# Moving a weight fold, reordering one down projection and unsharing the last norm in an eight-core encoder step

## The reference, cut to what matters

```python
# 1: mixer
proj = rmsnorm(x, g_mix_pre) @ w_in
merged = [group_rmsnorm(pool(proj)), group_rmsnorm(conv(proj))]
x = x + rmsnorm(merged @ w_out, g_mix_post)
# 2: cross-attention into 256 memory tokens, 4 heads of 256
q = rmsnorm(x, g_x_pre) @ w_q
p = softmax(q @ k.T / 16); o = p @ v
x = x + rmsnorm(o @ w_co, g_x_post)
# 3: MLP
hid = square(relu(rmsnorm(x, g_ff_pre) @ w_up))
x = x + rmsnorm(hid @ w_down, g_ff_post)
```

## Time and profile before

| what | us |
|---|---|
| time, median of 3 runs | 868.41 |
| lowest and highest of the 3 | 868.3, 869.23 |
| the profiled execution's own time | 868.5 |
| its span on the slowest core (core 2), first to last instruction | 867.0 |
| spans of the eight cores | 851.2 to 867.0 |
| PE busy on core 2 | 820.3 (95%) |
| DVE busy, ACT busy | 386.4, 386.5 (45% each) |

### The profile page before, as it was taken

One profiled execution on the slowest core, in us unless ns is written; L12 is line 12 of the kernel. 1 busy time (PEld: TensorE's weight loads), 2 busy tenths in 40 slices (PEclk: granted clock), 3 DMA queues, 4 the chain that ended last, 5 costly groups with the idle time before them and its releaser, 6 DMA issues.

```text
span 867.0 us, 13886 instructions; the slowest of 8 cores (851.2 to 867.0 us)
## 1 busy us (share of the span) xinstructions
PE 820.3 (95%) x4724; PEld 393.3 (45%) x4724; DVE 386.4 (45%) x526; ACT 386.5 (45%) x804; POOL 112.6 (13%) x192
## 2 busy tenths in 40 slices
PE   2979999999979999999998999999999999999995
PEld 0444454444445454445454445444444444444442
DVE  3796875667766556666223213231222321222112
ACT  3486775848656476566332223341323411233111
POOL 7735105206010000200010000000000000000000
PEclk9999999999989999999999999999999999999998
DMA  8999259640099325893889724982148920194001
GB/s 187 201 229 176 76 196 208 102 62 1 3 153 163 116 81 200 140 173 80 145 146 161 179 73 113 158 148 75 73 118 150 154 67 25 53 154 86 25 25 49
DMA packets 29793, 102.39 MB, mean 118 GB/s; under 512 B 2386, under 2 KB 13266, under 8 KB 24348
## 3 DMA queue, kind: packets, MB, share of 16 engines
q0 software_dynamic: 19696, 68.37, 45.7%
q1 hardware_dynamic: 9884, 33.01, 11.1%
q10 hardware_dynamic: 144, 0.13, 0.1%
HBM read 144.38 MB, written 18.07 MB: 187 GB/s over the span
## 4 chain that ended last, share of the span: by engine, by line
PE 81%; DMA 9%; DVE 3%; issue 3%; POOL 2%; ACT 1%; another core or an unknown queue 0%; DVEq 0%; SPq 0%; POOLq 0%; ACTq 0%
PE ps L657 79%; DMA wdn_139<-w_down 4%; PE ps L662 2%; DMA wco<-w_co 2%; DMA win<-w_in 1%; DMA up_130<-w_up 1%; POOL sAB_100 L695 1%; DMA X<-x 1%; DVE pld_103 L712 1%; POOL sAB_101 L695 1%; ACT rf_107 L686 0%; DMA yp<-X 0%; DVE z_98 L693 0%; DVE X L712 0%
## 5 line engine op out<-in xcount | busy, mean ns | idle before, releaser
L657 PE MATMUL ps<-xT_53,win 128*128 128x512 bf16 x256 | 63.1, 390 | 16.9 <-DMA win<-w_in 15.8
L693 DVE TENSOR_TENSOR O_55<-ps,gp 128x1024 f32<-128x1024 f32 (+1 forms) x25 | 29.4, 1178 | 95.8 <-PE ps L657 74.7
L693 DVE TENSOR_TENSOR O_56<-ps,gp 128x1024 f32<-128x1024 f32 x24 | 29.3, 1222 | 95.1 <-PE ps L657 59.0
L686 ACT ACTIVATE rt_128<-ps 128x512 bf16<-128x512 f32 x64 | 38.2, 597 | 71.2 <-PE ps L657 69.0
L686 ACT ACTIVATE rt_127<-ps 128x512 bf16<-128x512 f32 x64 | 38.2, 596 | 70.5 <-PE ps L657 68.7
L686 ACT ACTIVATE O_55<-ps 128x1024 f32<-128x1024 f32 (+2 forms) x27 | 25.4, 942 | 94.2 <-PE ps L657 89.8
L686 ACT ACTIVATE O_56<-ps 128x1024 f32<-128x1024 f32 (+1 forms) x25 | 24.9, 996 | 94.2 <-PE ps L657 92.8
L657 PE MATMUL ps<-xT_54,win 128*128 128x512 bf16 x256 | 59.6, 379 | 0.0
L657 PEld LDWEIGHTS ps<-xT_53,win 128*128 128x128 bf16 x256 | 24.5, 100 | 45.4 <-issue 21.9
L657 PE MATMUL ps<-xT_54,up_129 128*128 128x512 bf16 x192 | 42.4, 379 | 0.0
L657 PE MATMUL ps<-xT_53,up_130 128*128 128x512 bf16 x192 | 42.4, 379 | 0.0
(11 more groups left out here) (333 smaller groups left out, 1506.2 us busy)
## 6 DMA issues: line engine op xcount, KB each, us to landing
up_129<-w_up POOLq DMA_DIRECT2D x11, 1024.0 KB, 9.8
up_130<-w_up POOLq DMA_DIRECT2D x11, 1024.0 KB, 10.0
up_131<-w_up POOLq DMA_DIRECT2D x10, 1024.0 KB, 9.9
x<-X SPq DMA_DIRECT2D x16, 512.0 KB, 3.4
X<-x SPq DMA_DIRECT2D x16, 512.0 KB, 4.3
yp<-X SPq DMA_DIRECT2D x15, 512.0 KB, 2.7
X<-xp POOLq DMA_DIRECT2D x8, 512.0 KB, 44.1
X<-xp SPq DMA_DIRECT2D x8, 512.0 KB, 4.1
```

Source lines behind the costliest of these rows:

```text
L657: P.add([("pe", lambda e, L: e.matmul(L(out), lhsT=lhsT, rhs=rhs, start=start, stop=stop, skip_group_check=True), max(0.03, n * 0.000421 + ...
L686: return e.activation(out=L(out), in_=L(in_), func=func, scale=scale, **kw)
L693: opts.append(("dve", lambda e, L: e.tensor_tensor(out=L(out), in0=L(in0), in1=L(in1), op=op), c_dve(n, per)))
```

## The change

Five edits go together:

- `load_win(0)` is recorded ahead of the four XT loads.
- `fold_b` moves from ahead of the attention loop to behind the four `attn_head` calls of its first pass (`p == 0`).
- In tile 0 of the MLP `out_tile` gets `late=True`: for sub-tiles 0 and 1 the first 16 k-chunks (both halves) run first, then the remaining 16 of sub-tile 0, then those of sub-tile 1; k-chunks go outside, halves inside. Sub-tiles 2 and 3 run over all 32 in one go, in that same loop order.
- From the attention stage on, ACT's squares in `post` and `post_halves` are written to a bfloat16 buffer of their own (`sqj`, over se0 and se1) in place of O.
- In `post_halves` both adds into X are recorded first, then the two stores, the right half's on ACT's queue in place of SP's.

```diff
+    sqj = at("sqj", se[0].off, D, BF16)
...
+    late_stage = [False]
...
-        act(Ob, full, AF.Square, accum=ss)
+        act(sqj[0:r, :] if free_se else Ob, full, AF.Square, accum=ss)
...
-        act(half(Ob, 0), ps.v(0, 128, 0, 512), AF.Square, accum=s0)
+        act(half(sqj, 0), ps.v(0, 128, 0, 512), AF.Square, accum=s0)
...
-        act(half(Ob, 1), ps.v(0, 128, 512, 1024), AF.Square, accum=s1)
+        act(half(sqj, 1), ps.v(0, 128, 512, 1024), AF.Square, accum=s1)
...
             stt(half(X, h), half(Ob, h), rs, half(X, h), ALU.mult, ALU.add)
-            dma("sp", half(dst, h), half(X, h), 262144, wr=False)
+        for h in range(2):
+            dma(("sp", "act")[h], half(dst, h), half(X, h), 262144, wr=False)
...
-    def out_tile(t, chunks, nk, w, gp, dst):
+    def out_tile(t, chunks, nk, w, gp, dst, late=False):
+        tiles = {}
+        def part(i, k0, k1):
+            if i not in tiles:
+                tiles[i] = PS(2)
+            ps = tiles[i]
+            for kc, h in [(kc, h) for kc in range(k0, k1) for h in range(2)] if late else [
+                    (kc, h) for h in range(2) for kc in range(k0, k1)]:
+                mm(ps.v(0, 128, h * 512, (h + 1) * 512), chunks(kc)[:, i * 128:(i + 1) * 128], w(kc, h),
+                   kc == 0, kc == nk - 1)
+        if late:
+            for i in range(2):
+                part(i, 0, nk // 2)
         for i in range(NSUB):
...
+            part(i, nk // 2 if late and i < 2 else 0, nk)
+            ps = tiles[i]
...
-            post(ps, X, 128, gp)
+            post(ps, X, 128, gp, free_se=late_stage[0])
...
+    load_win(0)
     for i in range(4):
         load(XT[i], xt0[i], 524288, q=("sp", "pool")[i % 2])
-    load_win(0)
...
-    for m in range(8):
-        fold_b(m)
+    late_stage[0] = True
...
         step(None)
+        if p == 0:
+            for m in range(8):
+                fold_b(m)
...
-        out_tile(t, hid, 32, wd, gslot["g_ff_post"], yp)
+        out_tile(t, hid, 32, wd, gslot["g_ff_post"], yp, late=t == 0)
```

More of the change, by code:

```diff
@@ L594, in build_program @@
     sT = at("sT", hids.off, 512, rows=36)
+    sqj = at("sqj", se[0].off, D, BF16)
+    assert se[1].off == se[0].off + 1024
     A0 = cur[0]
@@ L799, in build_program, with post @@
     o_n = [0]
-    def post(ps, X, r, gp, out_x=None):
+    late_stage = [False]
+    def post(ps, X, r, gp, free_se=False):
         full = ps.v(0, r, 0, D)
@@ L865, in pre_first @@
         act(r0sq[:, :], ln, AF.Exp, scale=-1.0)
-    def out_tile(t, chunks, nk, w, gp, dst):
-        for i in range(NSUB):
[L869 to L873, removed]
+    def out_tile(t, chunks, nk, w, gp, dst, late=False):
[11 more added lines that the diff above has]
+                part(i, 0, nk // 2)
+        for i in range(NSUB):
+            part(i, nk // 2 if late and i < 2 else 0, nk)
+            ps = tiles[i]
             X = Xof[(t, i)]
```

## The result

| what | before | after |
|---|---|---|
| time, median of 4 runs each (us) | 868.36 | 857.79 |
| lowest to highest | 866.94 to 869.23 | 855.08 to 858.61 |
| ratio, 95% interval | | 0.9874 (0.9848 to 0.9901) |
| the profiled execution, its span | 868.5, 867.0 (core 2) | 858.61, 857.1 (core 6) |

The forecast was 857.1 with a range of 853.8 to 861.5. Total and sign came out; the terms less well, and that is what the experiments are about. In some executions, of the kernel before as of others, the cores of one die show a lower granted clock and the time grows (0.82 to 0.84 and 1006.87 us in one of run 9); these are left out of the times and ratios. In the changed kernel some lines stand three lower (`mm` is L660 instead of L657, `act` L689, `dma` L734) and tile numbers are one higher (wdn_139 is now wdn_140).

What follows compares the result with a forecast made beforehand. PE, busy for 95% of core 2's span, bounds the kernel; its long waits are for weights from DMA. Fold -6.7, down projection -2.8 and last norm -1.8 sum to -11.3; 868.5 - 11.3 - 0.1 = 857.1 us, range 853.8 to 861.5.

Steps and rivals of the forecast that it cites:

- The fold, -6.7: Fold behind pass 0's scores: the 4.50 us w_co wait goes and the 32 matmuls take 7.07 us, not 9.27.
- The hand-over: First attention output after the fold needs all 16 copies to Bm: cost taken as 0, ordinary upper end 0.88 us.
- that rival and the one on the other side: At the step to the first attention output: PE waits for Bm, 862.6 us, chance 0.12; slower, 870.4 us, chance 0.03.
- The late down projection, -2.8: Tile 0's down projection: 4.28 us of w_down waits shrink to one of 1.5 us, for wdn_139.
- The last norm, -1.8: Kernel's end: second add 2.29 us earlier, less 0.45 for overlapping stores; bounds a 2.3 gain and a 1.8 loss.
- The second queue: Second last store on ACT's queue: gives about nothing, the whole 1.8 us coming from the order of the adds.
- The squares' own buffer, 0: Last norm: the multiply still follows the square, as both read one PSUM bank; by the shared buffer alone -0.8 us.
- The start, 0: w_in part ahead of XT loads: r0 0.4 us earlier to 1.7 later; cost 0, up to 1.7 without cover.
- the cover named: PE's 3.1 us wait for w_out hides any slip of the start; expected to remain, between 1 and 4 us.
- better than the sum: Rival: w_out wait shrinks, PE keeps its clock, the 1.5 us before wdn_139 is filled: 853.4 to 854.9 us, chance 0.08.
- those four: Rivals: slow ACT queue, 861.2 us, 0.05; edits don't bite, 868.4, 0.04; hand-over wait, 862.6, 0.12; slower, 870.4, 0.03.
- sign of error: Signs: Bm wait over 1 us, last store above 3 us, start slipping beyond w_out wait, another slowest core with own waits.

Runs made afterwards that it cites:

- run 9: The change with the old load order and SP's closing list cut to transfers no engine had waited for, ACT's last: 854.21 us, ratio 0.9836.
- run 3: The kernel before with only fold_b moved behind the scores of pass 0: 861.02 us, ratio 0.9911.
- run 2: The change without the new load order, load_win(0) put back behind the XT loads: 857.4 us, ratio 0.9871.
- run 5: The kernel before with only the new end, both adds first and the second store from ACT: 867.49 us, ratio 0.9998.
- Run 7: The change with both last stores on SP's queue, the adds still ahead of them: 855.89 us, ratio 0.987.
- run 8: The change with the squares of post and post_halves written to O again: 857.83 us, ratio 0.989.
- run 1: The kernel before with only the new load order, load_win(0) ahead of the XT loads: 864.06 us, ratio 0.9947.
- run 11: The kernel before with the moved fold and the new load order together: 861.64 us, ratio 0.993.
- run 12: The kernel before with the moved fold and the late down projection together: 858.84 us, ratio 0.9893.
- run 6: The change with ACT's semaphores last in SP's closing list of waits: 854.98 us, ratio 0.9858.
- run 10: The change with SP's closing list cut as in run 9, the new load order kept: 855.66 us, ratio 0.9859.
- run 4: The kernel before with only the late order in tile 0's down projection: 864.98 us, ratio 0.9964.

## Why the prediction was right, and where it wasn't

**The fold, -6.7: right, a little low.** Alone it gave 7.7 us (6.6 to 8.9 by the interval). In run 3 the stretch from the state outputs to the first matmul on Bm takes 48.3 us on every core, against 54.75 on core 2 before: 6.4 us, about the term as forecast; attention's later passes got shorter too (108.2 us on core 1 of run 3, 110.8 on core 2 before). In the change the stretch lost 7.8. The 1.35 us beyond run 3 (48.31 less 46.96) belong to the new load order, 0.88 of it fold_a's two waits, which vanished because the planner then took most of fold_a ahead of the last mixer output. Run 2, with the old order, still has both, on core 4:

```profile
245.44 0.60 PE L660 MATMUL ps<-kT,wqT 128*128 128x256 bf16 x4 [0.30 <-DVE Am L725]
246.62 4.55 PE L660 MATMUL ps<-kT,wqT 128*128 128x256 bf16 x40 [0.58 <-DVE O L696]
```

The prediction took both waits for waits on copies. Only the 0.30 is one (to Am); the 0.58 is released by a DVE multiply that writes O, in the mixer's norm. The hand-over was taken at 0 and is 0; that rival and the one on the other side fell with it.

**The late down projection, -2.8: right, the wait a little high.** One wait is left, for the part that was named, and it is 0.89 us in place of 1.5. PE was at that point when forecast: 478.0 less the 5.74 us by which this stage begins earlier is 472.3, measured 473.27 - 0.89 = 472.4. The load came 0.6 us early: 479.5 - 5.74 = 473.8 against 473.2 (issued at 441.16, landed 32.0 later). Alone the edit gave 3.1 us.

**The last norm, -1.8: this is the term that was mis-sized.** It measured 0.45 in the traces and nothing in the times of run 5. Adds and stores did as the prediction said: adds at once, half stores of 2.0 and 2.1 us side by side. What failed is the step from "the store lands 1.8 us earlier" to "the program ends 1.8 us earlier". The prediction read the end as the landing of the last store. It was SP's closing list, which ran beside that landing before the change and begins behind it after. The 1.6 us from last landing to end of span could be worked out from rows 1, 11 and 12, and the loop stands in the code at L489 to L492; the prediction named SP's wait there and didn't ask what was queued behind it. With the list out of the way (run 9) the end is 3.3 us shorter than before, more than the 1.8 forecast and the 2.3 of the bound.

The second queue was counted as worth nothing by itself. The Trainium skill ("DMA: Bandwidth & Descriptors", section "Issuing engines are not separate DMA queues") says that spreading transfers over issuers saves issue time only. Run 7 agrees that there is nothing more to gain: with both stores on SP they are issued 0.81 us apart (850.19 + 1.14 - 0.33 = 851.00) and take 2.0 us each; with ACT's queue it is 0.80 us and 2.0 and 2.1. Nothing was gained by the queue, and its place in the list cost 1.6.

**The squares' own buffer, 0: right for the kernel before, 0.3 beside the new load order.** In run 8 the DVE multiply begins 0.79 us after the square (848.10 and 847.31), as in the changed kernel (849.52 and 848.73). The order is that of two readers of one PSUM bank, and the shared buffer didn't set it. The Trainium skill ("PSUM — Partial Sum Buffer", section Terms) calls two engines on one bank at once an error, reads against reads included. No run shows what would happen without the order. What did come back in run 8 stands behind the multiply, where the adds wait for ACT:

```profile
849.06 1.60 DVE L715 SCALAR_TENSOR_TENSOR X<-O,st,X 128x512 f32<-128x512 f32 x2 [0.27 <-ACT st L689]
```

The same 0.27 us stands in runs 1 and 11, which share O and have the new load order. It is not in runs 3, 5 and 12, which share O and have the old order, nor in the change. Why the two edits meet here is open.

**The start, 0: right as a sum, for another reason than the one given.** The sum of squares came late as forecast (its product at 23.21 us against 22.23, within the -0.4 to +1.7). But the cover named, the wait for w_out, shrank to 0.7 where 1 to 4 was forecast. In its place stand z (2.2 us on every core) and w_v:

```profile
151.48 3.62 PE L657 MATMUL ps<-wkv_109,mT_108 128*128 128x512 bf16 x16
```

```profile
154.22 6.20 PE L660 MATMUL ps<-wkv_110,mT_109 128*128 128x512 bf16 x16 [3.69 <-DMA wkv_110<-w_v]
```

```profile
wkv_109<-w_v POOLq DMA_DIRECT2D x1, 1024.0 KB, 17.9
```

```profile
wkv_110<-w_v POOLq DMA_DIRECT2D x1, 1024.0 KB, 22.9
```

These are PE's timeline of before (core 2) and after (core 6), then the DMA issues of both (last number: us to landing). PE comes there 0.95 us earlier (154.22 - 3.69 = 150.53), w_v is asked for 0.94 earlier (131.09 against 132.03 in POOL's timeline), but its transfer takes 5.0 us longer; so PE waits 3.69 us, and behind the wait runs 16 matmuls in 6.20 us instead of 3.62, at the clock of 0.55: 6.3 us at one place. PE had 0.95 of it in hand, and the waits for pld behind it shrink from 1.65 us to 0.36; that leaves 4.0, against the +3.6 in the table.

Over all cores the two parts of w_v take on average 18.9 to 20.3 us in the kernels with the new order (the change, runs 1, 6, 7, 8, 10, 11) and 17.2 to 18.1 in those with the old one (the kernel before, runs 2 to 5, 9, 12). Why they are slower there isn't settled; the DMA engines are full in both (busy share 1.01 after and 0.96 before between 130 and 150 us).

Over all eight cores this cost is met by a gain. From run 2 to the change, which has the new order, the state outputs begin 1.7 us later on average (226.87 in place of 225.21), and from there to the first matmul on Bm it takes 46.96 us in place of 48.31, on every core. That is the 1.35 us named under the fold, and it is why taking the new order back gained nothing in run 2.

Three pairs differ in this order alone, beside a moved fold: 0.9874 and 0.9871 (after, run 2), 0.9859 and 0.9836 (10, 9), 0.993 and 0.9911 (11, 3). Each leans to a cost, 0.3, 2.0 and 1.7 us; no pair settles it alone. That the same edit gains 4.6 us by itself is no contradiction: it shortens the wait for w_co and spares the clock behind it, which the moved fold removes anyway. The rival "better than the sum" saw the w_out wait shrink, but not what would follow.

**The rivals.** ACT's queue isn't slow (2.1 us), the planner kept the new orders, and PE waits nowhere for Bm; so those four fell. What the prediction named as a sign of error did come: a start that slipped beyond the w_out wait, and another slowest core with waits of its own.

**In sum** the total was right by luck, in that errors of both signs nearly cancelled. On the slowest cores the fold and the down projection gained 1.1 and 1.0 more than costed and attention's later passes, costed at nothing, 1.6; the end gained 1.4 less, and the mixer lost 3.6. Part of that 3.6 is only which cores are compared: in run 12, with the old order, the slowest core's state outputs begin at 229.36 us too.

## What to carry to other kernels

Follow the critical chain to the last instruction of the program: after the last transfer has landed, look which queue still has waits to work off, and put the latest transfer last among them. Edits that remove waits for loads need not add up to what each gives alone (run 11, though run 12 did): an edit that shortens a wait earns nothing beside one that removes it, and may only bring the next load's wait. When a wait is removed, ask of the next loads in line whether they keep their landing time, not only whether they are asked for earlier.

## What was not expected of the hardware

A wait that finds its semaphore already at its value isn't free on SP. In the changed kernel SP's own last store has landed at 853.1 us and ACT's at 854.0, so the rest of the list finds nothing left to wait for, and still takes 3.1 us: some 0.06 us for each of 51 waits (the expectations speak of some 64; 51 is what the code lists). Only the table of ends shows it; the view of waits has no row for it.

A wait of 2 to 3 us for w_v lowered PE's clock in one execution and not in another, and the longer wait is not the one that lowers it. Run 3 on core 7, then run 12 on core 6, first the wait in the timeline of each, then the stages behind it:

```profile
152.78 3.61 PE L657 MATMUL ps<-wkv,mT 128*128 128x512 bf16 x16 [2.73 <-DMA wkv<-w_v]
```

```profile
153.11 5.30 PE L657 MATMUL ps<-wkv,mT 128*128 128x512 bf16 x16 [2.04 <-DMA wkv<-w_v]
```

```profile
152.80:154.80 2.00, 2.00 (x10) 0.93 (x11) 0.62 (x2) 0.03 (x1) 1.37 (x2) 1.00 1.19 199
```

```profile
153.10:155.10 2.00, 1.99 (x6) 0.74 (x7) 0.81 (x1) 0.00 (x0) 2.00 (x3) 0.55 1.12 136
```

After 2.73 us the clock is 1.00 (2.4 GHz) and the 16 matmuls take 3.61 us; after 2.04 us it is 0.55, most of the stage at 1.2 GHz, and they take 5.30, with nearly the same matmuls ahead of either wait. What a wait costs through the clock can't be told here from its length alone.
